# A gated-linear-attention layer on one TensorE queue: the scores of a chunk directly behind its transposes, both half projections after them

## The reference, cut to what matters

```python
def step(s, blk):                       # per chunk; q, k: 4 heads x 128, v: 4 heads x 256
    qc, kc, vc, gc = blk
    b = jnp.cumsum(gc, axis=1)
    w = jnp.exp(where(causal, b[:, :, None] - b[:, None, :], -inf))
    scores = jnp.einsum('bihd,bjhd,bijhd->bhij', qc, kc, w)
    o = einsum('bhij,bjhe->bihe', scores, vc) + einsum('bihd,bhde->bihe', qc * jnp.exp(b), s)
    s = s * jnp.exp(b_last)[..., None] + einsum('bjhd,bjhe->bhde', kc * jnp.exp(b_last - b), vc)
proj = h @ w_in        # q, k, v, r and the low-rank gate
mix = (silu(r) * head_rms(o) * norm_w) @ w_out
```

## Time and profile before

| | |
|---|---|
| median of 3 runs | 2370.93 us (2370.62 to 2371.5) |
| the profiled execution | 2369.45 us, of it span of the instructions 2367.4 us |
| PE busy | 2348.8 us, 99% of the span |
| DVE, ACT, POOL busy | 55%, 33%, 51% |
| stretch of the GLA places | about 1170 to 1530 us from the start of the span |

### The profile page before, as it was taken

One profiled execution on the slowest core, in us unless ns is written; L12 is line 12 of the kernel. 1 busy time (PEld: TensorE's weight loads), 2 busy tenths in 40 slices (PEclk: granted clock), 3 DMA queues, 4 the chain that ended last, 5 costly groups with the idle time before them and its releaser, 6 DMA issues. The chain is left out here.

```text
span 2367.4 us, 45305 instructions
## 1 busy us (share of the span) xinstructions
PE 2348.8 (99%) x17800; PEld 2303.7 (97%) x17800; DVE 1299.5 (55%) x2039; ACT 790.3 (33%) x1252; POOL 1212.4 (51%) x1439
## 2 busy tenths in 40 slices
PE   9999999999999999999999999999999999999998
PEld 9999899999999999999999999999999999999998
DVE  6863254345545545556676776633444544544566
ACT  4701442222222222232454565622223223223224
POOL 2554146465665766666211112355476566566681
PEclk9999999999999999999999999999999999999999
DMA  4223031111111111112211112131111111111112
GB/s 165 65 65 92 28 131 41 50 41 50 51 39 49 50 45 45 54 46 104 80 47 66 57 46 75 49 120 45 45 45 46 55 45 45 49 51 45 45 56 83
DMA packets 41676, 142.48 MB, mean 60 GB/s; under 512 B 6448, under 2 KB 10160, under 8 KB 40336
## 3 DMA queue, kind: packets, MB, share of 16 engines
q1 hardware_dynamic: 32768, 106.78, 13.8%
q10 hardware_dynamic: 8720, 33.01, 4.0%
HBM read 120.42 MB, written 14.88 MB: 57 GB/s over the span
## 5 line engine op out<-in xcount | busy, mean ns | idle before, releaser
L766 PE MATMUL PS<-RB,WH 128*128 128x384 f32 (+1 forms) x4320 | 1069.6, 329 | 0.0
L766 PE MATMUL PS<-RA,WH 128*128 128x272 f32 (+2 forms) x3520 | 768.8, 308 | 2.9 <-DVE RA L1960 0.8
L766 PEld LDWEIGHTS PS<-RB,WH 128*128 128x128 f32 x4320 | 759.8, 188 | 5.4 <-issue 2.3
L766 PE MATMUL PS<-RB,WL 128*128 128x384 f32 (+1 forms) x2208 | 720.9, 327 | 0.0
L653 POOL TENSOR_TENSOR WH<-WR,FEW 128x256 fp32r<-128x256 f32 x416 | 321.7, 804 | 584.5 <-PE PS L766 555.7
L766 PEld LDWEIGHTS PS<-RA,WH 128*128 128x128 f32 x3520 | 585.9, 188 | 11.2 <-issue 4.3
L766 PE MATMUL PS<-RA,WL 128*128 128x272 f32 (+2 forms) x1760 | 540.5, 307 | 0.0
L766 PEld LDWEIGHTS PS<-RB,WL 128*128 128x128 f32 x2208 | 414.5, 188 | 0.0
L657 POOL TENSOR_TENSOR WL<-WR,WH 128x256 fp32r<-128x256 f32 x416 | 368.6, 916 | 0.0
L766 PEld LDWEIGHTS PS<-RA,WL 128*128 128x128 f32 x1760 | 330.7, 188 | 0.0
L2061 DVE TENSOR_TENSOR X<-PS,X 128x544 f32<-128x544 f32 x280 | 202.5, 724 | 204.2 <-PE PS L766 204.2
(11 more groups left out here) (243 smaller groups left out, 2253.7 us busy)
## 6 DMA issues: line engine op xcount, KB each, us to landing
WR<-ws SPq DMA_DIRECT2D x189, 512.0 KB, 3.4
EB<-xT ACTq DMA_DIRECT2D x8, 544.0 KB, 5.4
x_spill<-X ACTq DMA_DIRECT2D x8, 544.0 KB, 2.7
EB<-x_spill ACTq DMA_DIRECT2D x8, 544.0 KB, 6.4
GA<-st_gla ACTq DMA_DIRECT2D x4, 1024.0 KB, 4.8
glas_o<-GA ACTq DMA_DIRECT2D x4, 1024.0 KB, 4.6
yT<-X SPq DMA_DIRECT2D x16, 208.0 KB, 1.9
X<-xT ACTq DMA_DIRECT2D x4, 544.0 KB, 6.0
```

Of the source, the lines that this page charges most:

```text
L766: return nc.tensor.matmul(out, lhsT, rhs, start=start, stop=stop, skip_group_check=True)
```

## The change

In every place, the half projection that stood between `A` and `A2` of the next chunk moves behind `A2`. `A2` follows `A` directly on PE. In most places the moved half then stands directly in front of the second half, so that both run together between the scores and the outputs `B`. Where `L` is in the place, it stays between the two halves. DVE and ACT walk the same list; the moved item is a first half in 32 of the 35 places, at which neither DVE nor ACT takes anything out of PSUM. In the three places with p equal to 8 it is a second half, and there DVE's reading of the finished projection moves behind its selection of the scores.

```diff
             if not last:
-                s += (take(1) if p == 8 else []) + [("A",) + PLACES[k + 1]] + take(1)
-                s.append(("A2",) + PLACES[k + 1])
+                s += (take(1) if p == 8 else []) + [("A",) + PLACES[k + 1]]
+                s += [("A2",) + PLACES[k + 1]] + take(1)
                 if lines is not None:
```

## The result

The changed kernel takes 2388.15 us (median of 3 runs, 2388.12 to 2388.99) against 2370.93 us: 17.2 us slower, ratio 1.0072 with a 95% interval of 1.0058 to 1.0085. The forecast was 2385.1 us, the range 2381 to 2388.5. The profiled execution has a span of 2386.1 us, 18.7 more than that of before.

The account below looks back on a forecast made before the run. PE was taken as the bound, busy 2348.8 of 2367.4 us. Missed cover of 9.76 + 2.50 + 1.96 = 14.2 us, with seams and smaller waits at 0, on the median 2370.93 gave 2385.1 us, range 2381 to 2388.5.

Parts of the forecast that it names:

- The seams: PE's switches between transposes, scores, projection halves and outputs in 35 places: 5.42 against 5.43 us each, taken as 0.
- The cover: PE waits in the scores for DVE's level products once the half projection no longer hides them: 14.2 us added.
- eight named places: Head 0 chunks 3, 8; heads 1, 2, 3 chunks 3, 8: 9.76 us in five, 2.50 in two, 1.96 in one.
- the three heads' chunk 0: Chunk 0 of heads 1, 2, 3: level 0 ends 0.31 us before the scores would start, so nothing added.
- the read in front of it: DVE's read of the finished projection, starting its level chain at head 0 chunk 3 after idling 0.54 us for PE.
- The clock: Rival, 5%: PE's clock falls to 1.2 GHz after long idle, two halves cost 4.2 us more, 2393.5 us in total.
- the two deepest waits: The clock rival's two places with the deepest waits, head 2 chunk 8 the strongest: 8.4 us together.
- my own list of what would be wrong: Signs: L2581 over 1 us earlier, a seam over 0.1 us off, GLA clock under full, time outside the eight.
- Smaller waits: GLA stretch: up to 1 us may go, the same may be added by a late read; 0 in the sum.
- Rivals for no change: DVE's chain comes earlier with the scores, 2370.9 or 2368 us, 5%; seams pay 3.2 us, 2370 to 2374, 4%.

Follow-up runs that it names:

- experiment 1: Changed kernel with the 11 places first in their column group back in the old order, new order in the other 24: 2368.23 us, ratio 0.9987.
- experiment 5: Changed kernel with 16 unused transposes (12 at head 0 chunk 3) before the level 2 wait in four first places where the clock fell: 2384.18 us, ratio 1.0052.
- experiment 6: Changed kernel with 16 unused transposes (1.8 us) more in front of head 0 chunk 1, shifting everything behind later: 2390.17 us, ratio 1.0079.
- experiment 10: Changed kernel with first places in the old order and products of levels 2, 1, 0 ahead of `B` on DVE: 2367.61 us, ratio 0.9985.
- experiment 7: Kernel before with the new order in one place only, head 0 chunk 6: 2368.68 us, ratio 0.9988.
- experiments 3: Changed kernel, among first places new order only at head 0 chunks 3, 8, head 1 chunk 8, head 2 chunk 8: 2383.25 us, ratio 1.0051.

## Why the prediction was right, and what it missed

- **The seams.** Said: 5.42 against 5.43 us in a place, so nothing. Measured: 5.39 in the place shown, and experiment 1 with 24 new seams shows no step over 0.07 us beside the one explained. Whether transposes or a projection stand in front of the scores made no difference here.
- **The cover.** Said: half projection less slack, 14.2 us in eight named places. Measured: 14.1 us in the same eight, single terms within 0.05 us (by experiment 5, without anything subtracted, within 0.05 as well), and the three heads' chunk 0 and the other places at nothing. The reason it could be so close: five of the eight places already waited, so their term was a length, not a guess. DVE's chain did not move, as the read in front of it said (idle 0.48 for PE after, 0.54 before).
- **The clock.** This was a rival at 5%, and the one part that was badly judged. I tied it to the two deepest waits, with both halves slow, 8.4 us in all. It came together with the forecast in four places, also behind a wait whose longest piece is 0.67 us, shorter than the 0.79 us of the earlier trace rows that I had called safe. Each fall costs 1.55 us, as the clock comes back within the first half or shortly after, and the four together 6.2 us. A clock under full in the GLA stretch was on my own list of what would be wrong. The Trainium skill ("TensorE: Matmul & The Clock Gate", Part 1) ties the fall to idle time of TensorE; experiment 5 agrees, since work in the wait prevents it, and experiment 6 adds that equal waits differ. The fall in experiment 10 does not fit: no idle piece over 0.2 us stands in front of it.
- **The luck in it.** The time lies inside the range by 0.35 us, and two things of about 1.5 us each kept it there that stand at nothing in my sum: the smaller waits below, and the median of before, which already holds about one fall. Of the 6.2 us of the clock 3.1 were left to see, and the measured time is 3.05 us over the forecast. The mechanism of the 14.2 us is shown; that the time stayed in the range is luck. The range was also described wrongly: its lower end is 4.1 us under the forecast, not 3.
- **Smaller waits.** Said: up to 1 us may go. Measured: 1.5 us, most of it an idle piece marked as issue in the kernel before, which I had not listed though it is the second largest of the stretch. It was in fact the one real gain of the change (experiment 7).
- **Rivals for no change.** The chain does not come earlier with the scores (L2581 ends at 1199.61 and 1199.62), and the seams pay nothing.

## What to carry to other kernels

Before moving filling work from in front of a consumer to behind it, find the last producer's end for every place and price the move as the length of the filling less the slack; where the trace already shows a wait, the whole length is lost. On TensorE, add the clock to each new idle piece: here about 1.55 us each time it fell (2.4 once, where it stayed low twice as long), in four of the six places with a piece of 0.67 us or more in the changed kernel and in five of six in its shifted version, one profile each, and not predictable from the length. Look at the granted clock of every run of the kernel before too: its median may already hold such falls, and a comparison of medians then mixes them with what the change does. The right order was different by place: scores early where their inputs are long ready, late where they are not.

## What was not expected of the hardware

- Behind equal waits the clock fell or did not (longest piece 0.67 us at head 0 chunk 3: it fell in the changed kernel, not in experiments 3 and 6). Whether the moment decides or each run differs is open.
- The clock fell once with no idle piece over 0.2 us in front (experiment 10), behind 136 small matmuls.
- About 190 small matmuls in a row left PE idle for 1.05 to 1.7 us with no semaphore to wait for; 12 projection matmuls between them (2.1 us) took the idle time away. What it waits for is open.
